# Differential attention in a hybrid encoder layer: weights transposed and copied once, plain float32 product with V, six score banks, and squares of x three tiles ahead

## The chip, the core and the metric

The kernel runs on one core of one Trainium2 chip. It uses TensorE (PE; its weight loads are shown as PEld), VectorE (DVE), ScalarE (ACT), GpSimd (POOL) and the DMA queue of SyncE (SP). The metric is the device time of one execution in microseconds (us). Inputs and outputs are float32 in the chip's main memory.

## What is computed

One encoder layer over 2048 tokens of width 1024. Only the first two stages matter here:

```python
hn = rms_norm(h, g_mix)                       # over the 1024 columns
proj = hn @ w_in                              # q, k, v of group A and of group B
# group A: differential attention, 4 heads, two maps of 64 columns each, V has 128 columns
s = einsum('bhmqd,bhmkd->bhmqk', q * scale, k)
pr = softmax(s, axis=-1)
a = pr[:, :, 0] - lam * pr[:, :, 1]
o = einsum('bhqk,bhkd->bhqd', a, v)
o = rms_norm(o, subln_g, SUBLN_EPS) * (1.0 - lam_init)
# group B: dilated attention; then output projection, MLP, gate, final norm
```

## The kernel before

Six phases run one after the other, with a barrier of all engines between two of them. Each engine has a program of its own, written out by hand, and executes it strictly in that order; semaphores join the programs. A matmul in reduced float32 (float32r) loses low bits, so an operand is split into a high part (a rounded copy, made by ScalarE) and a low part (the rest, made by VectorE), and the parts are multiplied separately.

**Projection (`project_phase`, tensors `a_...`).** First two V stages of group A, then two of group B (`V_PAIRS`), 16 tiles of 128 tokens each, then q and k. In the first V stage x itself is still being prepared. For tile t: SP loads it (`load_x`, five slots), ScalarE squares and sums it (`square`), GpSimd makes the reciprocal root (`root`), VectorE scales it (`normalise`), TensorE turns it (`turn`, 8 transposes into `a_turned`), ScalarE and VectorE make `a_xt_hi` and `a_xt_lo` (`hi`, `lo`), and TensorE multiplies it with the weights (`values`, 24 matmuls into `a_acc`). ScalarE and VectorE take the result out in two parts (`v_hi` L260, `v_lo` L313) into `a_hl`, and SP stores it (`store_v` L189). ScalarE's order for tile t is `square(t + 5)`, `hi(t + 1)`, `v_hi(t)`. SP's is `load_x(t + 5)`, `store_v(t)`.

**Differential attention (`differential_phase`, tensors `c_...`).** 64 steps: 4 heads x 16 tiles of 128 queries. In a step, for each of two maps, TensorE makes scores against all 2048 keys in four PSUM banks of 512 (`score`, L760 and L761, k in a high and a low part). VectorE takes the maximum of each 1024 (`maximum` L630) and ScalarE the exponentials (`exp` L570, 1024 at a time, each followed by a read of its sum). VectorE combines the two maps into one row of weights, `a_row` (`combine` L667). TensorE transposes it in four groups of four (`turn_a` L770) into two PSUM banks. ScalarE copies the high part of each group (`a_hi` L577) and VectorE makes the low part (`a_lo` L673). TensorE multiplies both with V, which itself stands as high and low side by side in 256 columns (`values` L782, L783: 32 matmuls). ScalarE, VectorE and GpSimd then normalise the 128 x 128 result. Scores run up to two steps ahead of the product with V. A score bank pair is written again only when ScalarE has read it: `score` waits for `S["exp"]`.

Of the kernel before, what the change touches and what calls it, by code (L numbers as in the profile page):

```python
# [20 lines left out]
P = 128  # L21
# [70 lines left out]
def project_phase(kit):  # L92
# [13 lines left out]
    with ExitStack() as mem:  # L106
# [58 lines left out]

        def done_by(n):
            return (n + 1) * TILES if n < NV else V_UNITS + (n + 1 - NV) * BLOCKS * 2

        with nc.Block() as block:

            @block.sync
            def _(sp):
# [12 lines left out]
                def store_v(n, t):  # L185
                    kind, pair = V_PAIRS[n]
                    j = n * TILES + t
                    sp.wait_ge(v_lo_done, j + 1)
                    sp.dma_start(D["v"][kind, t * P:(t + 1) * P, pair * GROUP:(pair + 1) * GROUP],  # L189
                                 hl[:, j % 4].bitcast(F32)).then_inc(stored[j % 4], 16)  # L190
# [40 lines left out]
            def _(act):  # L231
# [22 lines left out]
                def v_hi(n, t):  # L254
                    j = n * TILES + t
                    act.wait_ge(acc_done, j + 1)
                    if j >= 4:
                        act.wait_ge(stored[j % 4], 16 * (j // 4))
                    d = (P, HD)[V_PAIRS[n][0]]
                    nc.scalar.copy(hl[:, j % 4].rearrange("p (h u d) -> p h u d", u=2, d=d)[:, :, 0],  # L260
                                   acc[:, j % BANKS, :PW].rearrange("p (h d) -> p h d", d=d)).then_inc(v_hi_done, 1)

                def qk_hi(i):
                    for ab in range(2):
                        act.wait_ge(rope_done, 2 * i + ab + 1)
                        act.wait_ge(stored[2 * ab], 16 * (V_UNITS // 4 + i))
                        nc.scalar.copy(hl[:, 2 * ab], prod[:, 2 * ab]).then_inc(rope_hi, 1)
# [25 lines left out]
            def _(dve):  # L293
# [14 lines left out]
                def v_lo(n, t):  # L308
                    j = n * TILES + t
                    d = (P, HD)[V_PAIRS[n][0]]  # L310
                    view = hl[:, j % 4].rearrange("p (h u d) -> p h u d", u=2, d=d)
                    dve.wait_ge(v_hi_done, j + 1)
                    nc.vector.tensor_tensor(view[:, :, 1], acc[:, j % BANKS, :PW].rearrange("p (h d) -> p h d", d=d),  # L313
# [14 lines left out]
                def qk_lo(i):  # L328
                    for ab in range(2):
                        dve.wait_ge(rope_hi, 2 * i + ab + 1)  # L330
                        dve.wait_ge(stored[2 * ab + 1], 16 * (V_UNITS // 4 + i))
                        nc.vector.tensor_tensor(hl[:, 2 * ab + 1], prod[:, 2 * ab], hl[:, 2 * ab].bitcast(F32),
                                                ALU.subtract).then_inc(rope_lo, 1)
# [19 lines left out]
            def _(pool):  # L353
# [93 lines left out]
def differential_phase(kit):  # L447

# [8 lines left out]
    STEPS = HEADS * TILES  # L457
    with ExitStack() as mem:
# [13 lines left out]
        qs = sb("qs", [P, 2, 2, HALF], F32R)  # L472
        v_hl = sb("v_hl", [P, 2, KT, 2, VD], F32R)
        mx = sb("mx", [P, 2])
        neg_max = sb("neg_max", [P, 2, 2])
        e = sb("e", [P, 2, 2, SEQ])
        sums = sb("sums", [P, 2, 2, 2])
        den = sb("den", [P, 2])
        rec = sb("rec", [P, 2])
        rec0 = sb("rec0", [P, 2])  # L480
        coef = sb("coef", [P, 1])
        a_row = sb("a_row", [P, 2, SEQ])
        at_hi = sb("at_hi", [P, 2, KT, P], F32R)
        at_lo = sb("at_lo", [P, 2, KT, P], F32R)
        o_part = sb("o_part", [P, VD])
        o = sb("o", [P, VD])
        o_junk = sb("o_junk", [P, VD])
        o_ssq = sb("o_ssq", [P, 1])
        o_part_mean = sb("o_part_mean", [P, 1])
        o_mean = sb("o_mean", [P, 1])  # L490
        inv_dim, eps = sb("inv_dim", [P, 1]), sb("eps", [P, 1])
        o_rstd = sb("o_rstd", [P, 1])
        o_unit = sb("o_unit", [P, VD])
# [7 lines left out]
        k_in, v_in, q_in, stored = (kit.sem_pair("c_" + s) for s in ("k_in", "v_in", "q_in", "stored"))  # L501
        names = ("scored mx negmax exp den rec coef kept a a_turned "
                 "a_hi a_lo a_lo2 pv part o ssq scaled mean rstd unit out")
        S = {name: kit.sem("c_" + name) for name in names.split()}

        with nc.Block() as block:

            @block.sync
            def _(sp):
# [3 lines left out]
                def load_q(m):  # L513
                    if m >= 2:
                        sp.wait_ge(S["scored"], 4 * 8 * (m - 1))
                    for k in range(4):
                        sp.dma_start(qs[32 * k:32 * k + 32, m % 2].bitcast(F32),
                                     rows(0, m // 2, k % 2, k // 2)[:, :, m % 2 * HALF:m % 2 * HALF + HALF]
# [9 lines left out]

                def load_v(h):
                    if h >= 2:  # L530
                        sp.wait_ge(S["pv"], TILES * (h - 1))
                    sp.dma_start(v_hl[:, h % 2].rearrange("p t u d -> p t (u d)").bitcast(F32),
                                 D["v"][0, :, h * 2 * VD:(h + 1) * 2 * VD].rearrange("(t p) d -> p t d", p=P)
# [8 lines left out]
                load_k(0)  # L542
# [3 lines left out]
                sp.dma_start(gain_in[:], D["g_subln"].partition_broadcast(P)).then_inc(const_in, 16)  # L546
                load_v(0)
                load_q(1)
                load_k(1)
                load_v(1)  # L550
                for n in range(STEPS + 3):
                    if n % 8 == 0 and n >= 8 and n // 8 + 1 < STEPS // 8:
                        load_q(n // 8 + 1)
# [1456 lines left out]
```

## Time and profile before

| | us |
|---|---|
| median of 3 runs | 3827.98 (3824.82 to 3831.37) |
| profiled execution, its own time | 3828.59 |
| its span, first to last instruction | 3826.8 |
| projection | 0 to 617 |
| differential attention | 617 to 1403.6 |

The profiled execution is at the median of the runs. Over the span TensorE is busy 90% of the time, VectorE 50%, ScalarE 35% and GpSimd 17%, with a mean granted TensorE clock of 0.963 of full speed. These shares are averages over phases that differ: in the differential phase VectorE is busier than TensorE. A matmul's record is longer than the time it keeps the next one waiting, so costs on TensorE are read from the distance between starts.

### The profile page before, as it was taken

The numbers are of one execution on the slowest core, as the hardware profiler recorded it, in microseconds if no ns is written. First come the engines' busy times: TensorE is split into PE (matmuls) and PEld (weight loads), VectorE is DVE, ScalarE is ACT, GpSimd is POOL, SyncE is SP. The second block draws the span as 40 slices with busy tenths as digits, with TensorE's granted clock in tenths as the row PEclk, the third lists the DMA queues.
The fourth block names the chain that finished last, engine by engine and source line by source line (L and its number), as shares of the span: only waits on it lengthen the run. The fifth ranks groups of instructions, "written<-read, shape, count | busy, mean of one in ns | idle before, by whom it ended". The sixth has DMA issues, their size and how long they took to land. (4 is left out here: it accounts for less than half of the span.)

```text
span 3826.8 us, 51496 instructions
## 1 busy us (share of the span) xinstructions
PE 3449.5 (90%) x18272; PEld 2961.5 (77%) x18272; DVE 1928.6 (50%) x3626; ACT 1338.3 (35%) x2814; POOL 658.1 (17%) x760
## 2 busy tenths in 40 slices
PE   5999995888888869999499799999999999998698
PEld 5998884677777759999377688888888888886587
DVE  3223343899999958887343333333343333332333
ACT  3211111666666647776122311212122112121333
POOL 2013331011111110000111121222211222111122
PEclk8999997999999989999799899999999999999899
DMA  4333336121210036774454511111141111112332
GB/s 139 129 109 115 121 121 171 45 49 52 61 39 18 6 85 148 165 165 114 159 177 143 198 52 46 47 52 44 51 152 45 54 44 49 50 44 80 126 107 93
DMA packets 276374, 351.12 MB, mean 92 GB/s; under 512 B 74608, under 2 KB 204528, under 8 KB 270960
## 3 DMA queue, kind: packets, MB, share of 16 engines
q1 hardware_dynamic: 276208, 348.97, 30.5%
q8 instruction: 96, 1.57, 0.2%
q14 instruction: 70, 0.57, 0.1%
HBM read 247.86 MB, written 101.06 MB: 91 GB/s over the span
## 5 line engine op out<-in xcount | busy, mean ns | idle before, releaser
L1589 DVE TENSOR_TENSOR e_h<-e_down_acc,e_h 128x512 f32<-128x512 f32 x512 | 350.5, 691 | 847.5 <-PE e_down_acc L89 847.5
L87 PE MATMUL e_up_acc<-e_xt_hi,e_up_hi 128*128 128x512 f32 x1024 | 399.2, 390 | 20.6 <-DVE e_xt_lo L1566 20.6
L88 PE MATMUL e_up_acc<-e_xt_lo,e_up_hi 128*128 128x512 f32 x1024 | 398.8, 389 | 0.0
L89 PE MATMUL e_up_acc<-e_xt_hi,e_up_lo 128*128 128x512 f32 x1024 | 398.8, 389 | 0.0
L87 PE MATMUL e_down_acc<-e_down_hi,e_u_hi 128*128 128x512 f32 x1024 | 398.3, 389 | 0.0
L88 PE MATMUL e_down_acc<-e_down_lo,e_u_hi 128*128 128x512 f32 x1024 | 398.3, 389 | 0.0
L89 PE MATMUL e_down_acc<-e_down_hi,e_u_lo 128*128 128x512 f32 x1024 | 398.3, 389 | 0.0
L630 DVE TENSOR_REDUCE c_mx<-c_scores 128x1 f32<-128x1024 f32 x256 | 306.0, 1215 | 67.1 <-PE c_scores L761 67.1
L570 ACT ACTIVATE c_e<-c_scores,c_neg_max 128x1024 f32<-128x1024 f32 x256 | 283.4, 1113 | 91.2 <-DVE c_neg_max L635 91.2
L1609 POOL TENSOR_TENSOR e_sq<-e_r 128x512 f32<-128x512 f32 x128 | 134.0, 1047 | 1006.4 <-ACT e_r L1545 1006.4
L760 PE MATMUL c_scores<-c_kt_hi,c_qs 128*128 128x512 f32 x512 | 218.5, 427 | 51.0 <-DMA c_gain_in<-g_subln_dram 37.1
L782 PE MATMUL c_pv<-c_v_hl,c_at_hi 128*128 128x256 f32 x1024 | 248.7, 284 | 0.9 <-issue 0.9
L1539 ACT CAST e_down_hi<-e_down_raw 128x2048 fp32r<-128x2048 f32 x32 | 61.2, 1913 | 537.9 <-PE e_down_acc L89 536.3
L783 PE MATMUL c_pv<-c_v_hl,c_at_lo 128*128 128x256 f32 x1024 | 242.9, 280 | 0.0
L87 PEld LDWEIGHTS e_up_acc<-e_xt_hi,e_up_hi 128*128 128x128 f32 x1024 | 192.6, 188 | 61.2 <-issue 20.9
L770 PE MATMUL c_turned<-c_ident,c_a_row 128*128 128x128 f32 x1024 | 147.3, 278 | 101.2 <-DVE c_at_lo L673 100.1
L1054 PE MATMUL b_scores<-b_kt,b_qs 128*128 128x256 f32 x768 | 207.0, 402 | 25.3 <-DMA b_masks<-masks_dram 25.3
L88 PEld LDWEIGHTS e_up_acc<-e_xt_lo,e_up_hi 128*128 128x128 f32 x1024 | 192.6, 188 | 39.9
L89 PEld LDWEIGHTS e_up_acc<-e_xt_hi,e_up_lo 128*128 128x128 f32 x1024 | 192.5, 188 | 40.0
L770 PEld LDWEIGHTS c_turned<-c_ident,c_a_row 128*128 128x128 f32 x1024 | 120.8, 142 | 132.3 <-issue 114.4
L89 PEld LDWEIGHTS e_down_acc<-e_down_hi,e_u_lo 128*128 128x128 f32 x1024 | 192.2, 188 | 39.9
L88 PEld LDWEIGHTS e_down_acc<-e_down_lo,e_u_hi 128*128 128x128 f32 x1024 | 192.2, 188 | 39.9
(169 smaller groups left out, 7811.0 us busy)
## 6 DMA issues: line engine op xcount, KB each, us to landing
s_qkt<-a_hl SPq DMA_DIRECT2D x128, 256.0 KB, 2.8
e_up_raw<-w_up_dram SPq DMA_DIRECT2D x32, 1024.0 KB, 5.8
e_down_raw<-w_down_dram SPq DMA_DIRECT2D x32, 1024.0 KB, 4.9
s_v<-a_hl SPq DMA_DIRECT2D x64, 256.0 KB, 2.0
b_kt<-s_qkt SPq DMA_DIRECT2D x64, 256.0 KB, 10.6
a_w_raw<-w_in_dram SPq DMA_DIRECT2D x24, 512.0 KB, 5.5
d_nd<-s_nd SPq DMA_DIRECT2D x48, 256.0 KB, 4.1
c_qs<-s_qkt SPq DMA_DIRECT2D x32, 256.0 KB, 5.0
```

The lines of the kernel that those rows point to most:

```text
L87: nc.tensor.matmul(out, lhs_hi, rhs_hi, start=first, stop=False)
L88: nc.tensor.matmul(out, lhs_hi, rhs_lo, start=False, stop=False)
L89: return nc.tensor.matmul(out, lhs_lo, rhs_hi, start=False, stop=last)
L570: nc.scalar.activation(e[:, s, m, f * HALF:(f + 1) * HALF], scores[:, 2 * f:2 * f + 2].rearrange("p b k -> p (b k)"), ACT.Exp, bias=neg_ma ...
L630: nc.vector.tensor_reduce(mx[:, f:f + 1], scores[:, 2 * f:2 * f + 2].rearrange("p b k -> p (b k)"), AX.X, ALU.max).then_inc(S["mx"], 1)
L760: nc.tensor.matmul(scores[:, b], queries, kt_hi[:, h % 2, m, cols], start=True, stop=False)
L770: ins = nc.tensor.transpose(turned[:, g % 2, c * P:(c + 1) * P], a_row[:, n % 2, (4 * g + c) * P:(4 * g + c + 1) * P], ident[:])
L782: nc.tensor.matmul(pv[:, :2 * VD], at_hi[:, s, c], v, start=(c == 0), stop=False)
L783: ins = nc.tensor.matmul(pv[:, :2 * VD], at_lo[:, s, c], v, start=False, stop=(c == KT - 1))
L1054: ins = nc.tensor.matmul(dst, queries, keys, start=(u == 0), stop=(u == 1))
L1589: nc.vector.tensor_tensor(h[:, slot(z, t), cols], down_acc[:, k % 4], h[:, slot(z, t), cols], ALU.add).then_inc(S["h"], 1)
L1609: nc.gpsimd.tensor_tensor(sq[:, k % 2], r[:, k % 2], r[:, k % 2], ALU.mult).then_inc(S["sq"], 1)
```

## The change

In the first V stage ScalarE now squares three tiles ahead, after `hi`, and V of group A is taken out by VectorE alone in one plain copy (half the bytes, array `vd`). The softmax scale moves from the exponentials into q and k, in instructions that were there already.

The differential phase is written anew. A step is cut into four quarters, one for each half row of keys of each map. Score banks: six (three pairs, `RING = 3`), so there is one `turned` bank and one `pv` bank. The transposed weights are copied once, as plain float32, by ScalarE (`a_copy`), and VectorE's `a_lo` is gone. V is plain float32: 16 matmuls of 128 columns with float32 operands in the place of 32 of 256 columns in float32r. `combine` is in two halves of 1024. The normalisation drops one ScalarE pass and moves the last product from GpSimd to VectorE. q is loaded in quarters of 512 columns instead of halves of 1024.

```diff
@@ projection, ScalarE
-                for t in range(2, X_SLOTS):
-                    square(t)
+                square(2)
                 split_w(1)
                 for n in range(NV):
                     for t in range(TILES):
                         if n == 0:
-                            if t + X_SLOTS < TILES:
-                                square(t + X_SLOTS)
                             if t + 1 < TILES:
                                 hi(t + 1)
-                        v_hi(n, t)
+                            if t + 3 < TILES:
+                                square(t + 3)
+                        if V_PAIRS[n][0]:
+                            v_hi(n, t)
@@ projection, VectorE
+                    if V_PAIRS[n][0] == 0:
+                        dve.wait_ge(acc_done, j + 1)
+                        if j >= 4:
+                            dve.wait_ge(stored[j % 4], 16 * (j // 4))
+                        nc.vector.tensor_copy(hl[:, j % 4, :PW].bitcast(F32), acc[:, j % BANKS, :PW]).then_inc(v_lo_done, 1)
+                        return
@@ projection, GpSimd
-                for t in range(2, X_SLOTS):
-                    root(t)
+                root(2)
                 split_w(1)
-                for t in range(X_SLOTS, TILES):
+                for t in range(3, TILES):
                     root(t)
@@ differential, tensors
+    RING = 3
+        v = sb("v", [P, 2, KT, VD])
+        at = sb("at", [P, 2, KT, P])
-        scores = ps("scores", [P, 4, 512])
-        turned = ps("turned", [P, 2, 512])
+        scores = ps("scores", [P, 2 * RING, 512])
+        turned = ps("turned", [P, 512])
@@ differential, ScalarE
+                def exp(n, u):
+                    m, f = UNITS[u]
+                    act.wait_ge(S["negmax"], 2 * n + m + 1)
+                    ...
+                def a_copy(n, g):
+                    act.wait_ge(S["a_turned"], n * 4 + g + 1)
+                    ...
+                    nc.scalar.copy(at[:, n % 2, 4 * g:4 * g + 4].rearrange("p c t -> p (c t)"), turned[:]).then_inc(S["at"], 1)
+                for n in range(-2, STEPS + 2):
+                    for q in range(4):
+                        if 0 <= n < STEPS:
+                            a_copy(n, q)
+                        if q == 0 and n >= 2:
+                            o_copy(n - 2)
+                        k, u = (n + 1, q + 2) if q < 2 else (n + 2, q - 2)
+                        if 0 <= k < STEPS:
+                            exp(k, u)
+                        if q == 0 and n >= 2:
+                            square(n - 2)
@@ differential, VectorE
+                for n in range(-2, STEPS + 2):
+                    for q in range(4):
+                        if n + 2 < STEPS:
+                            maximum(n + 2, q)
+                        if q == 0 and 0 <= n < STEPS:
+                            combine(n, 1)
+                        if q % 2 == 1 and n + 2 < STEPS:
+                            whole(n + 2, q // 2)
+                        if q == 1 and n >= 2:
+                            result(n - 2)
+                        if q == 2 and 0 <= n + 1 < STEPS:
+                            denominators(n + 1)
+                            reciprocal(n + 1)
+                            coefficient(n + 1)
+                        if q == 3 and 0 <= n + 1 < STEPS:
+                            combine(n + 1, 0)
@@ differential, TensorE
-                def score(n, m):
+                def score(n, u):
+                    m, f = UNITS[u]
+                    h, t, U = n // TILES, n % TILES, 4 * n + u
...
+                    if U >= RING:
+                        pe.wait_ge(S["exp"], U - RING + 1)
...
+                def turn(n, g):
+                    pe.wait_ge(S["a"], 2 * n + g // 2 + 1)
+                    pe.wait_ge(S["at"], 4 * n + g)
...
+                def values(n, g):
                     h, s = n // TILES, n % 2
-                    if side == 0:
+                    if g == 0:
+                        pe.wait_ge(S["o"], n)
...
+                    pe.wait_ge(S["at"], 4 * n + g + 1)
+                    for c in range(4 * g, 4 * g + 4):
+                        ins = nc.tensor.matmul(pv[:, :VD], at[:, s, c], v[:, h % 2, c], start=(c == 0), stop=(c == KT - 1))
+                    ins.then_inc(S["pv"], 1)
...
+                for n in range(-2, STEPS + 1):
+                    for q in range(4):
+                        if n + 2 < STEPS:
+                            score(n + 2, q)
+                        if 0 <= n < STEPS:
+                            turn(n, q)
+                        if 0 <= n - 1 < STEPS:
+                            values(n - 1, q)
```

The order of instructions at three places. First TensorE in the differential phase, before, from the second map's last scores of one step to the first product with V:

```order
L760 MATMUL c_scores<-c_kt_hi,c_qs 128x512
L761 MATMUL c_scores<-c_kt_lo,c_qs 128x512
L770 MATMUL c_turned<-c_ident,c_a_row 128x128 x12
L760 MATMUL c_scores<-c_kt_hi,c_qs 128x512
L761 MATMUL c_scores<-c_kt_lo,c_qs 128x512
...
L770 MATMUL c_turned<-c_ident,c_a_row 128x128 x4
L782 MATMUL c_pv<-c_v_hl,c_at_hi 128x256
L783 MATMUL c_pv<-c_v_hl,c_at_lo 128x256
```

Twelve transposes follow one block of eight score matmuls and four follow the next; 32 matmuls with V come after them. TensorE in the same phase of the changed kernel, one quarter and the start of the next:

```order
L739 MATMUL c_scores<-c_kt_hi,c_qs 128x512
L740 MATMUL c_scores<-c_kt_lo,c_qs 128x512
L739 MATMUL c_scores<-c_kt_hi,c_qs 128x512
L740 MATMUL c_scores<-c_kt_lo,c_qs 128x512
L747 MATMUL c_turned<-c_ident,c_a_row 128x128 x4
L758 MATMUL c_pv<-c_v,c_at 128x128 x4
L739 MATMUL c_scores<-c_kt_hi,c_qs 128x512
L740 MATMUL c_scores<-c_kt_lo,c_qs 128x512
```

Every quarter is four score matmuls, four transposes and four matmuls with V. ScalarE in the same phase, before:

```order
L577 CAST c_at_hi<-c_turned 128x512 x2
L570 ACTIVATE c_e,c_sums<-c_scores,c_neg_max 128x1024 x2
L577 CAST c_at_hi<-c_turned 128x512 x2
L590 ACTIVATE c_o_junk,c_o_ssq<-c_o 128x128
L570 ACTIVATE c_e,c_sums<-c_scores,c_neg_max 128x1024 x2
L595 ACTIVATE c_o_unit<-c_o,c_o_rstd 128x128
L584 ACTIVATE c_o_part<-c_pv,c_rec 128x128
```

And in the changed kernel, the last quarter of one step and the first two of the next:

```order
L591 COPY c_at<-c_turned 128x512
L583 ACTIVATE c_e,c_sums<-c_scores,c_neg_max 128x1024
L591 COPY c_at<-c_turned 128x512
L597 COPY c_o<-c_pv 128x128
L583 ACTIVATE c_e,c_sums<-c_scores,c_neg_max 128x1024
L604 ACTIVATE c_o_junk,c_ssq<-c_o 128x128
L591 COPY c_at<-c_turned 128x512
L583 ACTIVATE c_e,c_sums<-c_scores,c_neg_max 128x1024
```

One exponential now stands behind each copy of a turned group. Last, ScalarE in the first V stage, tiles 5 and 6 of the squares, before:

```order
L245 ACTIVATE a_junk,a_ssq<-a_rot 128x1024
L251 CAST a_xt_hi<-a_turned 128x4x128 x2
L260 CAST a_hl<-a_acc 128x2x128
L245 ACTIVATE a_junk,a_ssq<-a_rot 128x1024
L251 CAST a_xt_hi<-a_turned 128x4x128 x2
```

And in the changed kernel:

```order
L258 CAST a_xt_hi<-a_turned 128x4x128 x2
L252 ACTIVATE a_junk,a_ssq<-a_prod 128x1024
L258 CAST a_xt_hi<-a_turned 128x4x128 x2
L252 ACTIVATE a_junk,a_ssq<-a_prod 128x1024
L258 CAST a_xt_hi<-a_turned 128x4x128 x2
```

The square stands behind the copy instead of ahead of it, and is that of a tile two earlier; the copy out of `a_acc` is gone from ScalarE.

## Rows read from the trace of the kernel before

**Rows 1.** Windows: length, busy PE, PEld, DVE, ACT, POOL, granted clock, DMA share, GB/s.

```profile
17.00:90.00 73.00, 48.43 (x306) 46.41 (x307) 26.64 (x37) 24.21 (x49) 15.48 (x26) 0.84 0.34 115
...
645.00:665.00 20.00, 11.26 (x26) 7.38 (x27) 10.81 (x18) 7.00 (x13) 0.00 (x0) 0.59 1.05 259
...
1025.00:1210.00 185.00, 158.05 (x1035) 134.76 (x1036) 167.78 (x263) 124.38 (x262) 22.54 (x64) 1.00 0.23 57
```

**Rows 2.** Timeline, first V stage, one turn: start, us, engine, line, instruction, [idle before <-releaser].

```profile
48.66 0.43 SPq L176 DMA_DIRECT2D a_prod<-x_dram  x1
52.31 1.03 ACT L245 ACTIVATE a_junk<-a_prod 128x1024 f32<-128x1024 f32 x1 [4.94 <-DMA a_prod<-x_dram]
...
55.17 0.41 DVE L313 TENSOR_TENSOR a_hl<-a_acc,a_hl 128x256 fp32r<-128x256 f32 x1
```

**Rows 3.** Timeline, ScalarE, start and last five tiles of the first V stage.

```profile
20.64 1.05 ACT L238 CAST a_w_hi<-a_w_raw 128x1024 fp32r<-128x1024 f32 x1 [1.43 <-DMA a_w_raw<-w_in_dram]
...
107.26 0.37 ACT L260 CAST a_hl<-a_acc 128x256 fp32r<-128x256 f32 x1 [3.77 <-PE a_acc L89]
...
118.51 0.37 ACT L260 CAST a_hl<-a_acc 128x256 fp32r<-128x256 f32 x1 [2.23 <-PE a_acc L89]
121.39 0.37 ACT L260 CAST a_hl<-a_acc 128x256 fp32r<-128x256 f32 x1 [2.51 <-PE a_acc L89]
```

**Rows 4.** Groups of instructions, 700 to 1390 us: count, busy, mean ns, idle before.

```profile
L630 DVE TENSOR_REDUCE c_mx<-c_scores 128x1 f32<-128x1024 f32 x239 | 285.4, 1215 | 51.3 <-PE c_scores L761 51.3
...
L673 DVE TENSOR_TENSOR c_at_lo<-c_turned,c_at_hi 128x512 fp32r<-128x512 f32 x245 | 161.9, 681 | 2.5 <-ACT c_at_hi L577 2.5
```

**Rows 5.** Timeline of one step of the differential phase, at full clock.

```profile
941.06 2.34 DVE L667 SCALAR_TENSOR_TENSOR c_a_row<-c_e,c_coef 128x2048 f32<-128x2048 f32 x1
...
943.07 0.37 ACT L584 ACTIVATE c_o_part<-c_pv,c_rec 128x128 f32<-128x128 f32 x1
...
944.66 1.07 ACT L577 CAST c_at_hi<-c_turned 128x512 fp32r<-128x512 f32 x2 [1.23 <-PE c_turned L770]
...
946.66 0.63 PE L770 MATMUL c_turned<-c_ident,c_a_row 128*128 128x128 f32 x4 [1.60 <-DVE c_at_lo L673]
947.06 1.11 ACT L570 ACTIVATE c_e<-c_scores,c_neg_max 128x1024 f32<-128x1024 f32 x1
...
948.30 0.19 PEld L760 LDWEIGHTS c_scores<-c_kt_hi,c_qs 128*128 128x128 f32 x1 [0.28 <-ACT c_e L570]
...
949.33 0.60 PE L770 MATMUL c_turned<-c_ident,c_a_row 128*128 128x128 f32 x4
...
949.89 0.28 PE L783 MATMUL c_pv<-c_v_hl,c_at_lo 128*128 128x256 f32 x1
...
949.97 0.59 ACT L577 CAST c_at_hi<-c_turned 128x512 fp32r<-128x512 f32 x1 [1.24 <-PE c_turned L770]
...
952.41 2.35 DVE L667 SCALAR_TENSOR_TENSOR c_a_row<-c_e,c_coef 128x2048 f32<-128x2048 f32 x1
...
953.39 0.28 PE L783 MATMUL c_pv<-c_v_hl,c_at_lo 128*128 128x256 f32 x1
```

**Rows 6.** Timeline, first steps of the differential phase, at half clock.

```profile
644.90 0.29 PEld L760 LDWEIGHTS c_scores<-c_kt_hi,c_qs 128*128 128x128 f32 x1 [37.55 <-DMA c_gain_in<-g_subln_dram]
...
645.07 0.34 PEld L761 LDWEIGHTS c_scores<-c_kt_lo,c_qs 128*128 128x128 f32 x1
...
647.63 0.33 PEld L761 LDWEIGHTS c_scores<-c_kt_lo,c_qs 128*128 128x128 f32 x1
...
651.55 0.19 PEld L760 LDWEIGHTS c_scores<-c_kt_hi,c_qs 128*128 128x128 f32 x1 [3.58 <-issue]
...
667.90 1.74 PE L770 MATMUL c_turned<-c_ident,c_a_row 128*128 128x128 f32 x8
...
669.00 1.27 ACT L577 CAST c_at_hi<-c_turned 128x512 fp32r<-128x512 f32 x2 [3.69 <-PE c_turned L770]
```

**Rows 7.** Timeline, end of the differential phase, GpSimd.

```profile
1400.18 0.46 POOL L737 TENSOR_TENSOR c_out<-c_o_unit,c_gain 128x128 f32<-128x128 f32 x1 [0.51 <-ACT c_o_unit L595]
```

More of the change, by code:

```diff
@@ L457, in differential_phase @@
     STEPS = HEADS * TILES
+    UNITS = tuple((m, f) for m in range(2) for f in range(2))
+    QT = 4 * P
+    RING = 3
     with ExitStack() as mem:
@@ L500, in differential_phase, with bank @@
         lam_dots, half_set = kit.sem("c_lam_dots"), kit.sem("c_half_set")
-        k_in, v_in, q_in, stored = (kit.sem_pair("c_" + s) for s in ("k_in", "v_in", "q_in", "stored"))
-        names = ("scored mx negmax exp den rec coef kept a a_turned "
-                 "a_hi a_lo a_lo2 pv part o ssq scaled mean rstd unit out")
+        k_in, q_in, stored, v_in = (kit.sem_pair("c_" + s) for s in ("k_in", "q_in", "stored", "v_in"))
+        k0_in = kit.sem_pair("c_k0_in")
+        names = "scored halved negmax exp den rec coef a a_turned at pv o ssq eps mean rstd out"
         S = {name: kit.sem("c_" + name) for name in names.split()}
+        def bank(n, u):
+            b = (4 * n + u) % RING
+            return scores[:, 2 * b:2 * b + 2].rearrange("p b k -> p (b k)")
         with nc.Block() as block:
@@ L653, in coefficient, with combine @@
                                             ALU.mult, ALU.mult).then_inc(S["coef"], 1)
-                def keep(n):
-                    dve.wait_ge(S["rec"], n + 1)
-                    if n >= 2:
-                        dve.wait_ge(S["part"], n - 1)
-                        dve.wait_ge(S["o"], n - 1)
-                    nc.vector.tensor_copy(rec0[:, n % 2:n % 2 + 1], rec[:, 0:1]).then_inc(S["kept"], 1)
-                def combine(n):
-                    s = n % 2
+                def combine(n, f):
+                    s, cols = n % 2, slice(f * HALF, (f + 1) * HALF)
@@ L765, in turn_a @@
-                def turn_a(n, g):
-                    pe.wait_ge(S["a"], n + 1)
-                    if n * 2 + g - 1 > 0:
-                        pe.wait_ge(S["a_lo2" if g < 2 else "a_lo"], n * 2 + g - 1)
+                def score(n, u):
+                    m, f = UNITS[u]
+                    h, t, U = n // TILES, n % TILES, 4 * n + u
+                    if u == 0:
+                        pe.wait_ge(q_in[n // 4 % 2], 64 * (n // 8 + 1))
+                    if n == 0 and f == 0:
+                        pe.wait_ge(k0_in[m], 128)
+                    if h and t == 0 and u == 0:
+                        pe.wait_ge(k_in[h % 2], 128 * ((h + 1) // 2))
+                    if U >= RING:
+                        pe.wait_ge(S["exp"], U - RING + 1)
+                    queries = qs[:, n // 4 % 2, m, t % 4 * P:t % 4 * P + P]
+                    for b in range(2):
+                        cols = slice(f * HALF + b * 512, f * HALF + b * 512 + 512)
+                        found = scores[:, U % RING * 2 + b]
+                        nc.tensor.matmul(found, queries, kt_hi[:, h % 2, m, cols], start=True, stop=False)
+                        ins = nc.tensor.matmul(found, queries, kt_lo[:, h % 2, m, cols], start=False, stop=True)
+                    ins.then_inc(S["scored"], 1)
@@ L775, in values @@
                     h, s = n // TILES, n % 2
-                    if side == 0:
+                    if g == 0:
+                        pe.wait_ge(S["o"], n)
                         pe.wait_ge(v_in[h % 2], 16 * (h // 2 + 1))
-                        pe.wait_ge(S["o"], n)
-                    pe.wait_ge(S[("a_lo", "a_lo2")[side]], n * 2 + 2)
-                    for c in range(side * KT // 2, (side + 1) * KT // 2):
-                        v = v_hl[:, h % 2, c].rearrange("p u d -> p (u d)")
-                        nc.tensor.matmul(pv[:, :2 * VD], at_hi[:, s, c], v, start=(c == 0), stop=False)
-                        ins = nc.tensor.matmul(pv[:, :2 * VD], at_lo[:, s, c], v, start=False, stop=(c == KT - 1))
@@ L1223, in weigh @@
                     act.wait_ge(S["share"], a.n + START)
-                    nc.scalar.activation(weight[:], below[:], ACT.Exp, scale=SCALE).then_inc(S["weight"], 1)
+                    nc.scalar.activation(weight[:], below[:], ACT.Exp).then_inc(S["weight"], 1)
                 def m_hi(a):
```

316 lines of the change are left out of this document (111 added, 205 removed).

## The prediction

> **What bounds the kernel now.** I read the windows by phase first, then the groups, then single steps. In the differential phase VectorE is busy 167.8 us of 185, TensorE 158.1, ScalarE 124.4 [rows 1]. A step, read from `combine` to `combine`, takes 952.41 - 941.06 = 11.35 us [rows 5]. TensorE is not its own bound there: it waits 1.60 us for VectorE's `a_lo`, then 0.28 us for an exponential [rows 5]. VectorE carries four maxima at 1215 ns, four `a_lo` at 681 ns and one `combine` at 2.34 us [rows 4, 5]; `a_lo` alone is 2.7 us of the step by durations.
>
> The first V stage is bound by a loop through the x loads. SP issues the load for tile t+5 only after the store of tile t-1, at 48.66; the square of that tile starts at 52.31 after waiting 4.94 us for it; `hi`, `v_hi` and `v_lo` come behind it, and `v_lo` at 55.17 lets the next store and load go [rows 2]. The loop is some 7.4 us a tile. Once no load is left, tiles take (118.51 - 107.26) / 3 = 3.75 us, TensorE's own pace [rows 3].
>
> **The first V stage.** The square of tile t+3 needs a load issued about three tiles earlier. At 3.75 us a tile that is some 11 us; load to square took 3.65 [rows 2]. So the loop is cut and TensorE's 3.75 us is the pace. VectorE's work on a tile (normalise, two `lo`, one copy) is about 3 us and hides below it, as does the single plain copy in the place of a split. The start isn't shortened: both orders wait for the second weight slice, which ScalarE takes at 20.64 to 21.69 [rows 3]. From there I chain `hi(1)`, `square(3)`, `root(3)` (now behind GpSimd's weight split, costing a few us that were free), `normalise(3)` and `lo(2)`, and put `turn(3)` at about 27.5. Then 12 tiles of 3.75, and the last transposes (1.0) and two `values` (2.9 each): the last tile is out of TensorE at 79.3 to 80. Before, ScalarE took it at 121.39 [rows 3]. **Minus 41 us.** The remaining V stages and q and k keep TensorE full, so the smaller stores, the scale put into ScalarE's copy and VectorE's subtraction, and the dilated phase's lost scale are at nothing; if TensorE's cover were gone they would still be the same number of instructions of the same size.
>
> **The differential step: VectorE gets lighter.** It loses 2.7 us of `a_lo`, a small copy, and gets one more start of `combine`. About 8 us are left; by itself that would make TensorE the bound.
>
> **TensorE's work.** Scores are unchanged. The product with V: before, 32 matmuls of 256 columns start (953.39 - 949.89) / 30 = 0.117 us apart [rows 5], 3.73 us a step. After, 16 float32 matmuls of 128 columns. No float32 matmul stands in this trace; transposes are float32, but only move data. Lower bound: such a transpose, about 0.11 us each (four take 0.60, of which the last record is 0.28 long) [rows 5]. Upper bound: four of the 0.117 us matmuls with their weight loads, 0.467 us. I take 0.233 (two of them), the same 3.7 us a step as before, because two weight parts against two parts of 128 columns are as many loads and columns as before.
>
> The Trainium skill, page "FP8 and Floating Point Precision", section TensorE Precision Notes, says that true float32 takes four passes through the array. Four passes of 128 columns are 512 columns, which gives the same 3.7 us; no run here shows it yet.
>
> The sum of TensorE's work is then about 3.7 + 1.8 + 3.7 = 9.2 us, and if nothing waited the step would be 9.4.
>
> **But the new order closes a loop.** `score` number U waits for exponential U - 3 (`RING = 3`). In outer step n, quarter q, ScalarE runs the copy of turned group q and then exponential 4n + q + 6. TensorE's score of quarter q + 1 is U = 4n + q + 9 and waits for just that exponential. The copy in front of it waits for `turn(n, q)`, which stands on TensorE behind the score of quarter q. So every quarter is one chain: score, turn, copy, exponential, next score. Its parts from [rows 5]: the score's first weight load to the first transpose 949.33 - 948.30 = 1.03; first transpose to ScalarE's copy 949.97 - 949.33 = 0.64; one copy to the next start on ScalarE 0.48 (two take 1.07, one 0.59); exponential to the released score 948.30 - 947.06 = 1.24. Sum **3.39 us a quarter**. In the first quarter `o_copy` stands between copy and exponential: about 0.29 (the 128 x 128 copy out of PSUM lasts 0.37, and the next one starts a little sooner). Step: 4 x 3.39 + 0.29 = **13.85 us, 2.5 longer than before**.
>
> What hides in it: `values` starts 0.44 us after the turn and needs 0.93 of the 2.36 us until the next score, so it costs nothing up to 0.47 us a matmul. Only in the first quarter it waits for `o_copy`, starts 1.54 after the turn and must end by 2.65; room 1.0, need 0.93. VectorE needs at most 2.5 us a quarter: its maximum starts 1.2 after the score starts, and the maxima for an exponential were made a quarter earlier. Before, this chain was not closed: `exp` of both halves came before the copies they now stand behind, and `a_lo`, not `exp`, was the long wait.
>
> **The sum of the phase.** Before: first score 644.90, last product ends 1400.64, so 755.7 us [rows 6, 7]. After: until the first turn, eight scores of which five wait for an exponential. At half clock score matmuls start (647.63 - 645.07) / 6 = 0.427 us apart, a block is 1.7 us, and the first exponential lets go 6.65 us after the start, as now (651.55 - 644.90) [rows 6]; I get 19. Then 62 steps x 13.85 = 858.7. The last two steps have no scores (turn 0.64 + copy 0.62 + wake, or TensorE's 1.4 a quarter: 5.9 a step), then the last `values` 3.9 and the normalisation 2.6: 18.5. Sum 896. **Plus 140.5.** The first score comes earlier: 5 MB stand ahead of it in 27.9 us and half a megabyte of q goes: **minus 2.5**.
>
> Total: 3828.6 - 41 + 140.5 - 2.5 = 3925.6, made against the profiled execution, which lies 0.6 us above the median of the runs. Forecast **3926 us**.
>
> **The rivals.**
> 1. *Forecast*, the exponential behind the copy: 0.70. Own range 3900 to 3955 (0.2 us a step on the chain are 12; the first V stage and the phase's start 5 each).
> 2. *Dear float32.* At the upper 0.467 us a matmul the first quarter grows by about 0.85, the others not: 62 x 0.85 = 53, 3978. For it: no row shows such a matmul. Against: nothing but the count of columns. 0.10. A cheaper matmul changes nothing.
> 3. *The first V stage keeps its pace*, because another wait (GpSimd's root behind the weight split, or `lo` behind `normalise`) takes the load's place: 41 back, 3967. Against it: each needs about 3 us of 3.75. 0.06.
> 4. *The clock falls.* TensorE would idle 1 us in 3.4. The phase's start ran at a mean clock of 0.59 with idle stretches of 3.6 us [rows 1, 6]; with idle stretches of 1.6 us it was 1.00 [rows 1, 5]. At half clock the chain is 1.8 + (669.00 - 667.90) + 0.48 + 1.24 = 4.6 us, the step 18.8: 62 x 4.95 = 307, about 4230 if it lasted. The shorter idle stretches speak against it. 0.04. The Trainium skill, "TensorE: Matmul & The Clock Gate", Part 4 (PE-mode transpose), says that transposes don't count as busy for the clock. That would favour this rival; the trace held full clock with 16 of them in each step.
> 5. *The other side: the chain is shorter than I sum*, at one place, the ScalarE stretch from turn to released score (2.36 us). The kernel breaks even when 62 steps lose the remaining 97 us, a step of 12.3 us, a quarter of 3.0, that stretch at 1.97. If it fell to 1.4, TensorE's own work would bound: 9.4 a step, about 3650. For it: the copy is plain float32 now, and no row has this exact sequence. Against: every part was read between two starts. 0.10, of which 0.02 fall within 0.2% of no change.
>
> **How the numbers follow.** 0.2% (8 us) is about what a measurement of this kernel can tell from no change. Faster 0.08 and same 0.02 are rival 5; all others are slower: 0.90. The range must leave out at most 2 in 10: rivals 4 and 5 are 0.14, so it takes in 2 and 3: 3895 to 3980.
>
> **What the profile after would show.** If right: steps of 13.8 us; TensorE's score weight load with an idle of about 1 us ended by ScalarE's `c_e` in three quarters of four; ScalarE's copy waiting for `c_turned` in each quarter, busy near half; VectorE near 60%; granted clock near 1.00; V tiles 3.75 apart from about 30 us on and no square waiting for a load. Wrong, if the step is near 9.4 with TensorE never waiting for `c_e` (rival 5), if TensorE is busy without idle at over 13.9 a step (rival 2), if score matmuls start 0.43 apart (rival 4), or if the projection still ends at 617 (rival 3).

## The result: 2.45% slower, 3920 us, and the profile after

| | before | after |
|---|---|---|
| median (lowest to highest) | 3827.6 (3824.82 to 3831.37), 4 runs | 3919.71 (3918.76 to 3928.23), 4 runs |
| profiled execution, its own time | 3828.59 | 3918.96 |
| its span | 3826.8 | 3917.2 |
| differential attention, start to start of the next phase | 617.0 to 1403.6 | 574.0 to 1502.4 |

After over before is 1.0245, with a 95% interval of [1.0227, 1.0263]. The forecast was 3926 us.

The first part of the page of the changed kernel gives busy time, share of the span and number of instructions of each engine:

```profile
span 3917.2 us, 51666 instructions
...
PE 3456.1 (88%) x18272; PEld 2944.1 (75%) x18272; DVE 1801.1 (46%) x3370; ACT 1303.8 (33%) x2718; POOL 631.8 (16%) x694
```

No engine's share is higher than before. Shares over the whole span don't tell where the time went; the windows of the changed kernel do (columns as in [rows 1]):

```profile
17.00:81.00 64.00, 62.15 (x518) 61.57 (x518) 41.65 (x60) 31.81 (x58) 14.71 (x29) 1.00 0.43 136
575.00:625.00 50.00, 16.24 (x48) 10.64 (x48) 16.27 (x25) 10.59 (x20) 0.26 (x1) 0.65 1.03 232
800.00:1100.00 300.00, 222.14 (x1385) 182.98 (x1384) 181.72 (x261) 156.91 (x326) 23.57 (x66) 1.00 0.13 34
```

The first V stage is now filled by TensorE, 62.15 us of 64, where it was 48.43 of 73 [rows 1]. In the differential phase the busiest engine, TensorE, works 222 us of 300, and VectorE, formerly 167.8 of 185 [rows 1], 182 of 300: no engine is full, so the time is lost to waits. At the start of the phase the core waits for its loads, as before.

The pace of the tiles shows in the timeline of VectorE in the V stage of the changed kernel. These are the copies out of `a_acc` of two tiles in a row, and of the last one:

```profile
60.54 0.42 DVE L319 COPY a_hl<-a_acc 128x256 f32<-128x256 f32 x1 [0.93 <-PE a_acc L89]
64.28 0.42 DVE L319 COPY a_hl<-a_acc 128x256 f32<-128x256 f32 x1 [0.92 <-PE a_acc L89]
...
78.38 0.42 DVE L319 COPY a_hl<-a_acc 128x256 f32<-128x256 f32 x1 [2.46 <-PE a_acc L89]
```

Tiles are 3.74 us apart and the last one is taken out at 78.38, against 121.39 before [rows 3]: 43.0 us sooner.

Now one quarter of a differential step, and the quarter in which `o_copy` stands, from the timeline of the changed kernel (start, us, engine, line, instruction, idle before and its releaser):

```profile
999.80 0.19 PEld L739 LDWEIGHTS c_scores<-c_kt_hi,c_qs 128*128 128x128 f32 x1 [1.08 <-ACT c_e L583]
...
1000.83 0.60 PE L747 MATMUL c_turned<-c_ident,c_a_row 128*128 128x128 f32 x4
...
1001.27 1.06 PE L758 MATMUL c_pv<-c_v,c_at 128*128 128x128 f32 x8
1001.47 0.58 ACT L591 COPY c_at<-c_turned 128x512 f32<-128x512 f32 x1 [1.72 <-PE c_turned L747]
1001.95 1.12 ACT L583 ACTIVATE c_e<-c_scores,c_neg_max 128x1024 f32<-128x1024 f32 x1
...
1003.21 0.19 PEld L739 LDWEIGHTS c_scores<-c_kt_hi,c_qs 128*128 128x128 f32 x1 [1.08 <-ACT c_e L583]
...
1006.69 0.19 PEld L739 LDWEIGHTS c_scores<-c_kt_hi,c_qs 128*128 128x128 f32 x1 [1.14 <-issue]
...
1008.84 0.27 ACT L597 COPY c_o<-c_pv 128x128 f32<-128x128 f32 x1
1008.99 1.13 ACT L583 ACTIVATE c_e<-c_scores,c_neg_max 128x1024 f32<-128x1024 f32 x1
...
1009.16 1.16 PE L758 MATMUL c_pv<-c_v,c_at 128*128 128x128 f32 x8 [0.84 <-ACT c_o L597]
...
1010.27 0.19 PEld L739 LDWEIGHTS c_scores<-c_kt_hi,c_qs 128*128 128x128 f32 x1
```

Read it as a ring. The score starts at 999.80, the turn 1.03 later, ScalarE's copy 0.64 after that, the exponential 0.48 later, and 1.26 after its start the next score goes, after TensorE has waited 1.08 us. That is 3.41 us for a quarter. The two quarters behind it take 3.48 (to 1006.69) and 3.58 us (to 1010.27), the fourth 3.42. The step is 13.88 us over the whole phase, where it was 11.35. In the quarter with `o_copy` the product starts at 1009.16 and fills TensorE until 1010.27, just when the exponential would let go too (1008.99 + 1.26 = 1010.25).

The groups of the changed kernel from 700 to 1450 us (count, busy, mean ns, idle before and what ended it) say the same for 54 steps:

```profile
L630 DVE TENSOR_REDUCE c_neg_half<-c_scores 128x1 f32<-128x1024 f32 x217 | 265.9, 1225 | 290.5 <-PE c_scores L740 290.5
...
L758 PE MATMUL c_pv<-c_v,c_at 128*128 128x128 f32 x1731 | 234.2, 278 | 45.5 <-ACT c_o L597 45.5
...
L739 PE MATMUL c_scores<-c_kt_hi,c_qs 128*128 128x512 f32 x432 | 191.1, 442 | 149.0 <-ACT c_e L583 149.0
...
L591 ACT COPY c_at<-c_turned 128x512 f32<-128x512 f32 x217 | 126.9, 585 | 361.2 <-PE c_turned L747 361.2
```

TensorE's scores wait for ScalarE's exponential, ScalarE's copy waits for TensorE's turn, and VectorE's maximum, which had 51.3 us of idle ahead of it in 239 [rows 4], now has 290.5 ahead of 217. Three engines wait in turn for each other, and none is full.

The balance of the two profiled executions, by the starts of phases:

| | forecast | measured |
|---|---|---|
| start of the differential phase | -41 | -43.0 |
| from there to its first score | -2.5 | -2.6 (25.2 for 27.9) |
| first score to last result | +140.5 | +144.4 (900.1 for 755.7) |
| dilated attention | 0 | -1.2 |
| output projection | 0 | -11.0 (282.2 for 293.2) |
| the rest | 0 | +3.9 |
| own time | +97 | +90.4 |

The parts add up to +90.5; the last tenth is rounding. Before, the phase took 786.6 us, now 928.4.

### The profile page after: what moved, and what is told of

Read it like the earlier page. It is cut to its first block and busy times, and to the rows that moved or that the text cites. A ratio compares the mean times of both kernels' runs of the same rounds, so it can differ in the third digit from the quotient of the medians.

```text
span 3917.2 us, 51666 instructions
## 1 busy us (share of the span) xinstructions
PE 3456.1 (88%) x18272; PEld 2944.1 (75%) x18272; DVE 1801.1 (46%) x3370; ACT 1303.8 (33%) x2718; POOL 631.8 (16%) x694
## 5 line engine op out<-in xcount | busy, mean ns | idle before, releaser
L630 DVE TENSOR_REDUCE c_neg_half<-c_scores 128x1 f32<-128x1024 f32 x256 | 313.7, 1225 | 338.4 <-PE c_scores L740 338.4
L739 PE MATMUL c_scores<-c_kt_hi,c_qs 128*128 128x512 f32 x512 | 228.5, 446 | 214.4 <-ACT c_e L583 179.9
L758 PE MATMUL c_pv<-c_v,c_at 128*128 128x128 f32 x2048 | 276.4, 278 | 52.6 <-ACT c_o L597 52.6
L739 PEld LDWEIGHTS c_scores<-c_kt_hi,c_qs 128*128 128x128 f32 x512 | 96.8, 189 | 271.6 <-ACT c_e L583 145.4
L758 PEld LDWEIGHTS c_pv<-c_v,c_at 128*128 128x128 f32 x2048 | 248.3, 192 | 67.7 <-ACT c_o L597 67.7
L591 ACT COPY c_at<-c_turned 128x512 f32<-128x512 f32 x256 | 149.8, 585 | 422.6 <-PE c_turned L747 422.6
```

The costliest lines, as they stand in the source:

```text
L591: nc.scalar.copy(at[:, n % 2, 4 * g:4 * g + 4].rearrange("p c t -> p (c t)"), turned[:]).then_inc(S["at"], 1)
L630: nc.vector.tensor_reduce(neg_half[:, m, f:f + 1], bank(n, u), AX.X, ALU.max, negate=True).then_inc(S["halved"], 1)
L739: nc.tensor.matmul(found, queries, kt_hi[:, h % 2, m, cols], start=True, stop=False)
L758: ins = nc.tensor.matmul(pv[:, :VD], at[:, s, c], v[:, h % 2, c], start=(c == 0), stop=(c == KT - 1))
```

## The experiments

All ratios are to the kernel before, which was run again beside the experiments (median 3824.02 us for experiments 1, 2, 3 and 6, 3822.54 us for the others). "Changed kernel" is the one above, 3919.71 us.

**1. The exponential ahead of the copy.** If the ring sets the step, it opens when `exp` no longer stands behind `a_copy` on ScalarE. Nothing else is altered.

```diff
@@ differential, ScalarE
                     for q in range(4):
-                        if 0 <= n < STEPS:
-                            a_copy(n, q)
                         if q == 0 and n >= 2:
                             o_copy(n - 2)
                         k, u = (n + 1, q + 2) if q < 2 else (n + 2, q - 2)
                         if 0 <= k < STEPS:
                             exp(k, u)
+                        if 0 <= n < STEPS:
+                            a_copy(n, q)
```

> ScalarE's order alone is changed: in each quarter the exponential goes ahead of the copy of the turned group (and the copy of the result ahead of both). One turned bank, three score pairs, the float32 product and the V stage stay. Theory A (the chain score, turn, copy, exponential, next score sets the step): the exponential no longer waits for the turn of its quarter, the step falls from 13.88 to about 9.9 us, near TensorE's own work, 62 x 4.0 = 247 us less, about 3672 us. Rival B (the single turned bank or the float32 product sets the step): the order does nothing, 3919. Rival C (VectorE's maxima set it): 3919 or little less.

Measured: 3654.74 us (3654.37 to 3655.53), ratio 0.9562 [0.9537, 0.9588]. Two lines moved are worth 265 us, 18 more than expected. The timeline of VectorE's `combine` in this kernel, first halves of two steps, with a second half between them:

```profile
899.43 1.29 DVE L663 SCALAR_TENSOR_TENSOR c_a_row<-c_e,c_coef 128x1024 f32<-128x1024 f32 x1
901.77 1.28 DVE L663 SCALAR_TENSOR_TENSOR c_a_row<-c_e,c_coef 128x1024 f32<-128x1024 f32 x1
909.16 1.28 DVE L663 SCALAR_TENSOR_TENSOR c_a_row<-c_e,c_coef 128x1024 f32<-128x1024 f32 x1
```

The step is 909.16 - 899.43 = 9.73 us. The waits of the same kernel, 700 to 1200 us (engine, what it waits with, for whom, us in total, times, longest):

```profile
ACT c_at L591 <- PE c_turned L747: 77.9, 155, 0.7
...
PEld c_turned L747 <- DVE c_a_row L663: 45.5, 51, 0.9
```

The copy's mean wait falls from 361.2 / 217 = 1.66 us to 0.50 where it still waits, which is in three quarters of four, and TensorE no longer waits for an exponential at all. What is left of TensorE's idling is a wait for `combine`, once a step.

**2. The ring shortened on TensorE instead.** ScalarE's order stays; TensorE turns first and makes the scores behind it, which takes the 1.03 us of the score out of the ring.

```diff
@@ differential, TensorE
                     for q in range(4):
-                        if n + 2 < STEPS:
-                            score(n + 2, q)
                         if 0 <= n < STEPS:
                             turn(n, q)
+                        if n + 2 < STEPS:
+                            score(n + 2, q)
```

> TensorE's order alone is changed: in each quarter the four transposes go ahead of the score; ScalarE keeps copy ahead of exponential. Theory A: the turn leaves the chain from one exponential to the next score, so the chain loses the 1.0 us of the score between them; the step falls to about 11.4 us, 62 x 2.45 = 152 us less, about 3767 us. Rival B (turned bank, float32 product): no change, 3919.

Measured: 3758.34 us (3754.45 to 3760.29), ratio 0.9829 [0.9802, 0.9856]; a step of 11.25 us. Waits of this kernel, 700 to 1300 us:

```profile
ACT c_at L591 <- PE c_turned L747: 216.2, 213, 2.6
...
PE c_turned L747 <- DVE c_a_row L663: 98.7, 54, 1.8
```

The scores' wait for the exponential is gone here too. Three turns of a step start 2.25 to 2.5 us behind the one before, and the first stands 1.8 us and waits for `combine`, with the score queued behind it. Both swaps, on two engines, break the same ring; this shows that it was the ring and not one slow instruction.

What sets the step now is a second, longer ring, through VectorE, once a step. In one step of this timeline the fourth score starts at 809.06, and VectorE, which waited for it, starts the last maximum behind it:

```profile
810.27 1.23 DVE L630 TENSOR_REDUCE c_neg_half<-c_scores 128x1 f32<-128x1024 f32 x1 [0.46 <-PE c_scores L740]
...
811.61 1.29 DVE L663 SCALAR_TENSOR_TENSOR c_a_row<-c_e,c_coef 128x1024 f32<-128x1024 f32 x1
...
812.96 0.66 PE L747 MATMUL c_turned<-c_ident,c_a_row 128*128 128x128 f32 x4 [1.83 <-DVE c_a_row L663]
```

`combine` stands behind that maximum, the first turn behind `combine`, and the fourth score of the next step behind that turn. The same path holds TensorE up once a step in experiment 1, for less; experiments 7 and 8 go at it.

**3. The plain float32 product made dearer.** In the changed kernel each matmul with V is issued twice, so that the product with V is doubled.

```diff
@@ differential, values
+                        nc.tensor.matmul(pv[:, :VD], at[:, s, c], v[:, h % 2, c], start=(c == 0), stop=False)
-                        ins = nc.tensor.matmul(pv[:, :VD], at[:, s, c], v[:, h % 2, c], start=(c == 0), stop=(c == KT - 1))
+                        ins = nc.tensor.matmul(pv[:, :VD], at[:, s, c], v[:, h % 2, c], start=False, stop=(c == KT - 1))
```

> Every float32 matmul with V is issued twice into the same accumulation, so the product is doubled: TensorE has 3.7 us more work a step. Theory A: in three quarters of four it hides in the idle time ahead of the score; only the first quarter, where the product waits for the copy of the last result, grows by about 0.75 us: step about 14.6, 3968 us. Rival B (the float32 product sets the step): each of four quarters grows by 0.93, step 17.6, about 4150 us.

Measured: 3969.34 us (3968.39 to 3970.29), ratio 1.0385 [1.0349, 1.042]; a step of 14.57 us, 0.69 longer. The window of this kernel:

```profile
800.00:1100.00 300.00, 281.38 (x1987) 247.17 (x1986) 173.04 (x250) 149.28 (x308) 21.32 (x60) 1.00 0.13 32
```

Sixteen matmuls more are some 3.7 us of work a step at the 0.233 of the prediction, and the step grows by 0.69: four fifths lie in the ring's gap. 62 steps of 0.69 are 43 of the 50 us. Most of the rest is at the end of the phase, where no scores hide the product: from the last score's weights to the last result it is 33.3 us there and 23.3 in the changed kernel.

**4. And made cheaper.** Every second matmul with V is left out, so half of the product isn't computed.

```diff
@@ differential, values
-                    for c in range(4 * g, 4 * g + 4):
-                        ins = nc.tensor.matmul(pv[:, :VD], at[:, s, c], v[:, h % 2, c], start=(c == 0), stop=(c == KT - 1))
+                    for c in range(4 * g, 4 * g + 4, 2):
+                        ins = nc.tensor.matmul(pv[:, :VD], at[:, s, c], v[:, h % 2, c], start=(c == 0), stop=(c == KT - 2))
```

> The changed kernel with every second float32 matmul with V left out (half of the weights' product is not computed): TensorE has 1.9 us less work a step. Theory A (the product hides ahead of the next score): the step stays 13.88, 3917 to 3920 us. Rival B (the float32 product is what made the step longer): 62 x 1.9 = 115 us less, about 3805 us.

Measured: 3919.95 us (3919.5 to 3920.4), ratio 1.0253 [1.0233, 1.0274]. The window of this kernel:

```profile
800.00:1100.00 300.00, 184.35 (x1033) 143.97 (x1034) 181.67 (x260) 156.48 (x326) 23.44 (x66) 1.00 0.13 33
```

TensorE does 38 us less in 300, and the time is the same; the differential phase alone takes 928.1 us for 928.4. In the changed kernel this half of the new product costs nothing at all.

**5. The same half left out with the ring open.** Experiment 1 with the edit of experiment 4.

> The same half of the product left out, but with the exponential ahead of the copy (step 9.72 there). Theory A: with the chain open TensorE's work is nearly the whole step, so the same cut now counts: about 1.1 us a step by my sum of the engines' orders (VectorE's row is then waited for), 62 x 1.1 = 68 us less, about 3587 us. If the product costs nothing in itself: 3655 us.

Measured: 3601.2 us (3598.21 to 3604.19), ratio 0.942 [0.94, 0.9439], so 53.5 us less than experiment 1. The edit that was worth nothing in the ring is worth 53.5 us outside it; it removes 8 matmuls of 0.23 us, 1.8 us of a step, and 53.5 / 62 = 0.86 came back as time. That is less than the 1.1 us a step that was expected. Its waits from 700 to 1200 us say what took part of the rest: TensorE's weight loads wait 1.32 us a step for `combine`, where it was 45.5 / 51 = 0.89 in experiment 1, and 0.28 for an exponential, for which they did not wait there:

```profile
PEld c_turned L747 <- DVE c_a_row L663: 74.1, 56, 2.0
...
PEld c_scores L739 <- ACT c_e L583: 14.7, 53, 0.3
```

**6. The squares' order alone.** The kernel before, with nothing but ScalarE's squares and GpSimd's roots moved as in the change; V is still taken out in two parts.

```diff
@@ projection, ScalarE (kernel before)
-                for t in range(2, X_SLOTS):
-                    square(t)
+                square(2)
                 split_w(1)
...
-                            if t + X_SLOTS < TILES:
-                                square(t + X_SLOTS)
                             if t + 1 < TILES:
                                 hi(t + 1)
+                            if t + 3 < TILES:
+                                square(t + 3)
```

> The kernel before with one part of the change: squares three tiles ahead and behind the copies, the roots on GpSimd in the same order. Nothing else. Theory A (a load and square in the tile loop set the first V stage): about 43 us less than before, 3785 us. Rival B (the gain came from VectorE's single copy, which took a ScalarE step out of the tile loop): clearly less than that, 3800 to 3828 us.

Measured: 3783.24 us (3772.1 to 3790.46), ratio 0.9895 [0.9861, 0.9929]. The timeline of ScalarE in this kernel, end of the first V stage:

```profile
69.25 0.37 ACT L260 CAST a_hl<-a_acc 128x256 fp32r<-128x256 f32 x1 [1.18 <-PE a_acc L89]
...
72.99 0.37 ACT L260 CAST a_hl<-a_acc 128x256 fp32r<-128x256 f32 x1 [2.22 <-PE a_acc L89]
...
79.61 0.37 ACT L260 CAST a_hl<-a_acc 128x256 fp32r<-128x256 f32 x1 [2.51 <-PE a_acc L89]
```

3.74 us a tile and the last at 79.61, with the differential phase starting at 575.25 for 617.0: the gain of the first V stage is that of the squares' place. The four runs of this kernel lie 18 us apart, so these starts say it better than the medians. The single plain copy of V adds at most the 1.2 us by which the changed kernel is earlier still. The rest of the change costs 3919.71 - 3783.24 = 136 us: the differential phase takes 928.4 us for 784.3, 144 more, and later phases give some of it back.

**7. With the ring open, the product ahead of the turn.** Experiment 1, and TensorE runs score, values, turn, so that `combine` has one product longer to end.

```diff
@@ differential, TensorE (on experiment 1)
-                        if 0 <= n < STEPS:
-                            turn(n, q)
                         if 0 <= n - 1 < STEPS:
                             values(n - 1, q)
+                        if 0 <= n < STEPS:
+                            turn(n, q)
```

> The exponential ahead of the copy, and on TensorE the product ahead of the transposes in each quarter. With the exponential ahead of the copy TensorE still waits 0.5 to 0.9 us a step for VectorE's first half row. The product ahead of the transposes gives VectorE that time: step 9.72 to about 9.35, 62 x 0.35 = 22 us less, about 3633 us. Rival: the turned group then comes later to ScalarE and the copy holds up the next exponential, 3655 us or more.

Measured: 3633.38 us (3630.55 to 3636.99), ratio 0.9505 [0.9489, 0.9521]; a step of 9.29 us. Against experiment 1 the time that VectorE gets is worth 21 us, as expected.

**8. With the ring open, `combine` ahead of the maximum.** Experiment 1, and VectorE runs the first half of `combine` before the fourth maximum instead of behind it, where a maximum that waits for its scores kept it.

```diff
@@ differential, VectorE (on experiment 1)
                     for q in range(4):
+                        if q == 3 and 0 <= n + 1 < STEPS:
+                            combine(n + 1, 0)
                         if n + 2 < STEPS:
                             maximum(n + 2, q)
...
-                        if q == 3 and 0 <= n + 1 < STEPS:
-                            combine(n + 1, 0)
```

> The exponential ahead of the copy, and on VectorE in the last quarter the first half of the row ahead of the maximum. It goes at the same wait of TensorE for the row from the other side: the step falls from 9.72 to TensorE's own work, 9.1 to 9.2, 62 x 0.55 = 34 us less, about 3620 us. Rival: the maximum comes 1.2 us later and holds up the exponential and through it a score: no gain, 3655 us.

Measured: 3627.73 us (3624.78 to 3629.84), ratio 0.9491 [0.9475, 0.9507]; a step of 9.24 us. TensorE's wait for `combine` was 45.5 us in 51 steps in experiment 1. The waits (700 to 1200 us) of this kernel:

```profile
PEld c_turned L747 <- DVE c_a_row L663: 1.4, 1, 1.4
```

And a window:

```profile
800.00:1100.00 300.00, 299.89 (x2079) 266.63 (x2078) 272.00 (x392) 236.32 (x485) 39.36 (x96) 1.00 0.24 57
```

TensorE is busy 299.89 us of 300: the phase is all but bound by its work. (Records of matmuls overlap and hide short gaps: turns start 2.26 us apart in three quarters and 2.47 in one, and four times 2.26 would be 9.04.) This is the fastest version, 5.1% below the kernel before and 292 us below the changed one, with the same instructions as the changed one.

## Why the prediction was right

**The step that decided it, the closed ring, held.** Its parts were read from a kernel in which they did not form a ring, and in the quarter shown each came within 0.02 us: 1.03, 0.64, 0.48 and 1.26, where 1.24 was taken. The step is 13.88 us for 13.85. Opening the ring at either of two places removes the loss (experiments 1 and 2).

**"`values` costs nothing up to 0.47 us a matmul."** Experiment 4 shows it in the cheaper direction. Experiment 3 issues each matmul twice, which is the case of 0.467 us a matmul: three quarters of the step hide it, as stated, and for the first the prediction put 0.85 us a step and 53 in all (rival 2); measured were 0.69 and 50.

**Small parts were wrong, and cancel.** `o_copy` adds 0.15 us between copy and exponential, not 0.29, and in that quarter the product, for which the prediction had 0.07 us of room left, ends together with the ring. The exponential was short by 0.02 in each of four quarters, and one quarter was longer by another 0.07, which I had not foreseen. That the step came out within 0.03 us is in this part luck. The 18.5 us of the end were also added up too high: their own terms give 18.3.

**The float32 matmul, rival 2.** In the changed kernel's group of L758 the count is 1731 in 54 steps, 32 a step, for 16 matmuls: each float32 matmul of 128 columns leaves two weight loads and two matmul records, and eight records at 1001.27 span 1.06 us with the last 0.28 long, so (1.06 - 0.28) / 7 = 0.11 us apart. A matmul costs 0.22 us in this row, for 0.233 taken. Rival 2 fell. The Trainium skill, page "FP8 and Floating Point Precision", section TensorE Precision Notes, speaks of four passes for true float32. The duration agrees: four passes of 128 columns are 512 columns, and a score matmul of 512 columns starts 0.23 us behind the one before it. The rows show two records and not four.

**The first V stage, rival 3.** 43.0 us for 41: the pace of 3.75 held (3.74 measured), and the last tile came at 78.4 and not 79.3 to 80. Experiment 6 shows the squares' order as the cause.

**The clock, rival 4.** The granted clock is 1.00 (2.4 GHz) from 625 to 1500 us with TensorE idle 1.1 us in each quarter; at the phase's start, with the core waiting for its loads, it is 0.65. Rival 4 fell:

```profile
625.00:1500.00 875.00, 646.00 (x4048) 533.25 (x4048) 521.77 (x748) 452.90 (x944) 68.31 (x191) 1.00 0.10 26
```

The Trainium skill, page "TensorE: Matmul & The Clock Gate", Part 4 (PE-mode transpose), says that a transpose doesn't count as busy for the clock in the same way as other matmuls. No run here sets transposes apart; with 16 of them in a step and those gaps the clock did not fall.

**Rival 5, a shorter chain,** fell with the ring's measured parts. What it named as the other end, a step of 9.4 us bound by TensorE and about 3650 us, is nearly experiment 8's 9.24 and 3628: the sum of TensorE's work, 9.2, was right, and it became the bound once no ring was closed.

**Where the total is off.** Measured against forecast, own times: -2.0 in the first V stage, +3.9 from the first score of the differential phase to its last result (2.0 from the step, 2.1 from the last two steps, which took 20.6 us for 18.5, -0.2 from the start), -8.3 in later phases. The last is the largest miss, and it was no step of the prediction: I had later phases at nothing (-1.2 in the dilated attention, -11.0 in the output projection, and +3.9 behind it, 3.1 of which in the last phase, which I did not follow). That the sum is off by 6.6 us only is again in part misses of opposite sign.

**The largest miss: the clock in the output projection.** This phase takes 282.2 us for 293.2. Windows over it without its start and end, before and after:

```profile
1881.60:2109.00 227.40, 203.47 (x950) 167.60 (x949) 97.27 (x182) 50.65 (x103) 41.73 (x42) 0.95 0.48 164
```

```profile
1979.20:2193.00 213.80, 194.72 (x945) 158.91 (x943) 95.26 (x180) 49.41 (x103) 41.49 (x42) 1.00 0.50 172
```

About as many matmuls, at a clock of 1.00 instead of 0.95. Before, the granted clock is not low throughout: it falls to the half level (1.2 GHz) in six short stretches. Two windows of the kernel before, the 3.4 us ahead of the first of them and the stretch itself:

```profile
1922.00:1925.40 3.40, 1.44 (x13) 1.13 (x11) 1.48 (x4) 1.96 (x4) 3.02 (x3) 1.00 0.34 131
...
1925.40:1928.80 3.40, 3.40 (x13) 2.92 (x12) 2.52 (x3) 1.32 (x3) 0.03 (x1) 0.51 0.96 337
```

Ahead of it TensorE had little but transposes and stood 1.96 us waiting for GpSimd's `d_mixed`; in it, matmuls start 0.43 us apart instead of 0.23. The start and the end of the phase run at half clock in every profile. Between them, the length of the phase goes with the number of such stretches in all ten:

| stretches of 3.4 us at half clock | output projection, us |
|---|---|
| none (changed kernel, experiments 1, 5, 8) | 282.2, 282.8, 280.8, 282.8 |
| one (experiments 3, 7) | 283.8, 284.5 |
| three (experiments 2, 4) | 285.5, 287.0 |
| six (kernel before, experiment 6) | 293.2, 292.3 |

Six stretches at half clock lose 6 x 3.4 / 2 = 10.2 us of full-speed work, an estimate from these rows, and 11.0 were measured. So the clock accounts for nearly all of this difference, and it isn't fixed by the new phase: experiments 2 and 4 have the new phase, and experiment 4 the changed kernel's step too, with three stretches. The four runs of the changed kernel differ in a like way, three at 3918.8 to 3920.5 us with a mean granted clock of 0.972 to 0.974 and the fourth at 3928.23 with 0.970, though only one of them has a trace. What decides how many of these stretches a run has is open; both kernels with six have the old phase.

## What to carry to other kernels

In a kernel of in-order engines, a ring buffer's wait is only as good as what stands ahead of the releasing instruction: for every such wait, write down what precedes the releaser on its own engine and what that waits for, and if the path comes back to the waiting engine within one turn, its sum is the pace as soon as it is longer than each engine's own work in that turn, however idle the engines look. Opening one ring can leave the next (experiment 2). Durations for that sum can be read from start to start in a kernel where the ring is not closed. Making an instruction lighter pays only after that: here half of the product with V was worth 0 us in the ring and 53.5 outside it, and one swap of order 265.

## What the hardware showed that I had not expected

- A float32 matmul of 128 columns stands in the trace as two weight loads and two matmul records (1731 matmul records in 54 steps of 16 matmuls), some 0.11 us apart.
- TensorE idled about 1.1 us between stretches of work of 2.3 us, in three quarters of four, at a granted clock of 1.00 from 625 to 1500 us.
- The output projection took 280.8 to 293.2 us, by how many stretches of 3.4 us TensorE ran at half clock in it (none to six). Ahead of the first of them TensorE had done 1.44 us of transposes in 3.4 us. What decides their number is open.
